# Down halves of the experts issued by ScalarE on a second hardware queue in a one-core decoder step

## The reference, cut to what matters

```
(jax.nn.silu(xb @ w_g[e]) * (xb @ w_u[e])) @ w_d[e]
```

## Time and profile before

| what | value |
|---|---|
| median of 3 runs | 2143.52 us (2139.1 to 2146.24) |
| the profiled execution: its own time | 2136.13 us |
| span of the profiled execution, first to last instruction | 2134.2 us |
| PE busy in the span | 1816.0 us, 85% |
| ACT busy in the span | 279.2 us, 13% |
| queue q1 (SP) | 520.24 MB, 64.1% of the 16 engines' span |
| queue q0 (software, POOL) | 17.05 MB, 2.3% |
| queue q10 (ACT) | 6.33 MB, 1.4% |

### The profile page before, as it was taken

How to read it: one execution, slowest core, us unless ns; L and a number is a source line. 1 busy time by engine, 2 the same in 40 slices (tenths; PEclk the granted TensorE clock), 3 DMA queues, 4 the chain that set the end, 5 groups by cost and what they waited for, 6 DMA issues and landing times.

```text
span 2134.2 us, 22022 instructions
## 1 busy us (share of the span) xinstructions
PE 1816.0 (85%) x8780; PEld 1134.8 (53%) x8780; DVE 614.8 (29%) x1129; ACT 279.2 (13%) x537; POOL 271.1 (13%) x188
## 2 busy tenths in 40 slices
PE   7798999998788999993999897979979887787770
PEld 6687888887367888882543433434334332232320
DVE  6900699652535400006401101011010110110116
ACT  4001211103641210013000000000000000000002
POOL 0641222211910100001000000000000000000000
PEclk9899999999999999995999999999999998999995
DMA  5144111345934243316399999999999999999957
GB/s 227 60 119 118 66 67 71 118 177 168 6 126 192 79 158 123 114 60 262 117 406 392 403 410 409 406 397 406 398 414 384 400 414 408 409 409 405 403 214 294
DMA packets 91139, 544.81 MB, mean 255 GB/s; under 512 B 27984, under 2 KB 40784, under 8 KB 44400
## 3 DMA queue, kind: packets, MB, share of 16 engines
q1 hardware_dynamic: 70512, 520.24, 64.1%
q0 software_dynamic: 5888, 17.05, 2.3%
q10 hardware_dynamic: 14656, 6.33, 1.4%
HBM read 522.81 MB, written 37.26 MB: 262 GB/s over the span
## 4 chain that ended last, share of the span: by engine, by line
PE 60%; DMA 25%; DVE 9%; ACT 4%; issue 1%; SPq 1%; ACTq 0%; POOL 0%; DVEq 0%; POOLq 0%
PE psum L570 30%; DMA arena<-w_up_in 22%; PE psum L897 8%; PE psum L862 7%; PE psum L855 4%; PE psum L858 4%; PE psum L838 2%; PE psum L664 1%; PE psum L776 1%; DMA arena<-y_rows 1%; DMA arena<-v_cache_in 1%; DVE arena L1662 1%; SPq L487 1%; DVE arena L1759 1%; DVE arena L1488 1%
## 5 line engine op out<-in xcount | busy, mean ns | idle before, releaser
L570 PE MATMUL psum<-arena 128*128 128x260 f32 x3328 | 746.5, 387 | 32.8 <-DVE arena L1293 14.7
L570 PEld LDWEIGHTS psum<-arena 128*128 128x128 f32 x3328 | 640.5, 193 | 135.5 <-issue 25.8
L862 PE MATMUL psum<-arena 128*64 128x512 f32 x832 | 402.6, 642 | 113.4 <-DMA arena<-w_up_in 113.3
L864 PE MATMUL psum<-arena 128*64 128x512 f32 x832 | 403.4, 643 | 0.0
L862 PEld LDWEIGHTS psum<-arena 128*64 128x64 f32 x832 | 119.5, 148 | 377.4 <-issue 377.4
L897 PE MATMUL psum<-arena 128*64 128x512 f32 (+1 forms) x1024 | 269.9, 597 | 17.7 <-ACT arena L1113 17.0
L897 PEld LDWEIGHTS psum<-arena 128*64 128x64 f32 (+1 forms) x1024 | 94.0, 147 | 170.8 <-issue 148.2
L1727 DVE TENSOR_TENSOR arena<-arena,psum 64x512 f32<-64x512 f32 x26 | 18.0, 691 | 493.5 <-ACT arena L1110 493.5
L1225 POOL DMA_INDIRECT y_rows<-arena x32 | 30.1, 941 | 990.4 <-DVE arena L1736 990.4
L1736 DVE COPY arena<-psum 64x512 f32<-64x512 f32 (+1 forms) x64 | 43.5, 687 | 274.8 <-PE psum L897 274.0
L864 PEld LDWEIGHTS psum<-arena 128*64 128x64 f32 x832 | 119.5, 148 | 0.0
(11 more groups left out here) (313 smaller groups left out, 1288.1 us busy)
## 6 DMA issues: line engine op xcount, KB each, us to landing
arena<-w_gate_in SPq DMA_DIRECT2D x64, 2048.0 KB, 38.3
arena<-w_up_in SPq DMA_DIRECT2D x64, 2048.0 KB, 42.2
arena<-w_down_in SPq DMA_DIRECT2D x64, 2048.0 KB, 41.2
arena<-w_in_in SPq DMA_DIRECT2D x32, 1024.0 KB, 4.8
arena<-w_out_in SPq DMA_DIRECT2D x16, 1024.0 KB, 4.7
arena<-k_cache_in SPq DMA_DIRECT2D x8, 1024.0 KB, 6.9
arena<-v_cache_in SPq DMA_DIRECT2D x8, 1024.0 KB, 4.8
arena<-y_rows SPq DMA_DIRECT2D x4, 2048.0 KB, 19.1
```

The costliest lines, as they stand in the source:

```text
L570: last = mm(pair(n)[:, h, :], w(kk), rhs(kk)[:, HALF * h:HALF * (h + 1)], start=(kk == first), stop=(kk == kn - 1 and stop))
L862: lastg = mm(ps[0:SLIM, 2, :], xt[:, 8 * hf + kk, :], wg[:, kk, :], start=(hf == 0 and kk == 0), stop=(hf == 1 and kk == 7))
L864: lastu = mm(ps[SLIM:P, 2, :], xt[:, 8 * hf + kk, :], wu[:, kk, :], start=(hf == 0 and kk == 0), stop=(hf == 1 and kk == 7))
```

## The change

The down halves of places 2 to 31 are no longer issued by SP. SP's loop issues only the gate and up halves (`range(4)` instead of `range(6)`). ACT gets a new function `load_down(i)`: it waits until the first gate and up halves of place i - 1 are used (`s_half`, the same condition as in `load_next`), loads the expert's number from `ord_i` into a register, and issues both down halves into the same ring slots as before, with the same semaphores. ACT calls it for place i + 1 at the start of its work on place i, ahead of the Silu of place i, and waits once for `s_ord` before its loop. Places 0 and 1 are loaded by SP as before, and the loads of overflow blocks too. Slots, sizes, sources and the order of use on PE are unchanged.

```diff
@@ SP
             for i in range(2, NE):
                 e = sp.value_load(ord_i[0:1, ORDER[i]:ORDER[i] + 1], min_val=0, max_val=NE - 1)
-                for j in range(6):
+                for j in range(4):
                     load_next(6 * i + j, e)
@@ ACT
+            def load_down(i):
+
+                slots = slots_of(i)[0]
+                act.wait_ge(s_half, i)
+                e = act.value_load(ord_i[0:1, ORDER[i]:ORDER[i] + 1], min_val=0, max_val=NE - 1)
+                src = t["w_down"][bass.ds(e, 1)].rearrange("o (k p) n -> p (o k) n", k=4)
+                for j in range(2):
+                    act.dma_start(half_d(slots[4 + j]), src[:, 2 * j:2 * j + 2, :]).then_inc(s_ring[slots[4 + j]], 16)
+
+            act.wait_ge(s_ord, 1)
             for i in range(NE):
+                if 2 <= i + 1 < NE:
+                    load_down(i + 1)
                 expert(i, WIDE[i])
             overflow(act, lambda it: expert(it + NE, True))
```

## The result

The changed kernel takes 2155.51 us (median of 5 runs, 2152.52 to 2159.46) against 2143.52 before: 12 us more by the medians. The ratio of the two sets of runs is 1.0061, 95% interval 1.004 to 1.0081, that is 13 us (8.6 to 17.4). The prediction was 2154, in a range of 2136 to 2169. The profiled execution took 2154.18 us; that of before, 2136.13, is among the quickest of its kernel, so the profiles differ by more (18 us) than the medians.

The account below looks back on a forecast made before the run. Transfers were taken to bound the kernel, with PE following. SP 0, ACT 0, order at the end +9.2 and clock +1.2 summed to +10.4 us, giving 2154 us from a median of 2143.5, range 2136 to 2169.

Parts of the forecast that it names:

- The bound: Expert part, 1060 to 2036 us: transfers are the limit, engines busy at share 1.01 and 404 GB/s, PE following.
- 1% mark: Expert part: the prediction would be wrong if the transfer rate moved by 1% or more.
- SP, 0: SP's loop: dropping 60 issues and 30 waits gains 0, as the queue behind is full.
- ACT, 0: ACT before each Silu: added wait, register load and two issues, 0.9 to 1.3 us, are covered, costing 0.
- The middle: Places before the end: down halves competing from q10 cost nothing that lasts, as late engines stay fed.
- Down halves land early by at most two halves: Middle places: so a pair comes at most 10.4 us later, which the ring's depth of about eight halves absorbs.
- The order at the tail, +9.2: Last place: the gate and up pair lands last, at 2066.0 instead of 2056.8 us, costing 9.2 us.
- once and not per place: Middle places: a pair's delay of at most 10.4 us arises a single time, without adding up over places.
- The clock, +1.2 out of 0 to 2.3: PE's restart at the last pair: slow clock after idling costs 0 to 2.3 us, taken as 1.2.
- Same: Rival at the end: the last pair does not land last, tail costs 0 to 6 us; chance 0.21.
- Faster: Rival in the expert part: two hardware queues raise the rate, 2125 us at 416 GB/s; chance 0.14.
- much slower: Rival in the expert part: two queues on an engine cost rate, 2189 us at 390 GB/s; chance 0.12.

Follow-up runs that it names:

- e9: Kernel before, ACT given only the change's waits and register loads, no issues, all halves on SP; 2142.84 us, 1.0003 of the kernel before.
- e3: Changed kernel, ACT also issuing the second gate and up pairs of places 2 to 31; 2149.95 us, 1.0019 of the kernel before.
- e6: Kernel before, ACT given the change's waits, register load and two tiny issues per place, all weights on SP; 2147.15 us, 1.0023 of the kernel before.
- e5: Kernel before, all on SP's one queue, last place's down halves issued ahead of its second pair; 2155.44 us, 1.0065 of the kernel before.
- e1: Changed kernel, but the last place's down halves issued by SP again, behind its gate and up halves; 2147.68 us, 1.0017 of the kernel before.
- e11: Kernel of e10 with the whole change on top; 2129.2 us, 0.9958 of the kernel before.
- e12: Kernel of e10 with the change for places 2 to 30, last place's down halves on SP; 2121.4 us, 0.9917 of the kernel before.
- e7: Changed kernel with four unused matmuls on PE ahead of the last place's second pair; 2154.14 us, 1.0058 of the kernel before.
- e10: Kernel before, rows of nine slim experts moved to positions and partitions 64 to 127, in lists of 128; 2112.31 us, 0.985 of the kernel before.
- e4: Changed kernel with nine unused matmuls on PE ahead of the last place's second pair; 2158.08 us, 1.0063 of the kernel before.

## Why the prediction held, and where it did not

- **The bound.** Right as a whole. The share stays at 1.00 and the rate of 401 GB/s is inside the 1% mark that I set; e9, which moves no transfer, has 402.
- **SP, 0.** Right: it is freed of its long issues and nothing gains from it. The rate does not gain by a second issuing engine either (401 GB/s, and 402 in e3, against 404). The order of arrival, taken from rows, was worth 9 us and more.
- **ACT, 0.** The two issues take 0.91 to 1.8 us, mostly 0.92 (0.9 to 1.3 expected), and are over 4 us or more before the next Silu. e9 shows no price of waits and register loads. e6 leaves up to 8 us in doubt for the issues, which the 0 did not allow for.
- **The middle.** The total came out as argued, but not quite for the reason given: the engines did not always stay fed (share 0.97 in 1460 to 1560 us), and down halves were awaited, 27.3 us, which I had named as a sign of being wrong. The step that failed is "Down halves land early by at most two halves". With a third of the time for q10 I had worked out 31 us for the two, and a place takes 31.1, so there was no air; they land after 33.9 us (median). Of the two values that I left open, a third or a half, the profile is nearer to the half where both queues have work: in 2036 to 2050 us q10 holds 51.7% of the engines' time and q1 47.4%. It cost little, a few us at most, for the transfers set the pace.
- **The order at the tail, +9.2.** Right in mechanism and size. e5 makes the loss by the order alone; taking one place out of the change wins back 0.44% (e1), 9.4 us, and e11 less e12 is 7.8. By landings the pair came 9.9 us ahead of the last down half before, 9.2 being read from the windows. The text held that a pair comes two halves later "once and not per place". The profiles of e1 and e12 suggest that this once is paid at whatever pair PE has too few waits left behind, so that sparing the last place does not make it free.
- **The clock, +1.2 out of 0 to 2.3.** Mis-sized in the profiled execution: the restart came at the upper bound, 2.3 us, after 4.42 us of idle. e7 shows the same 2.3 saved when PE is kept busy, but no run shows it in the medians. The slow down matmuls (1.6 us more) were not foreseen and are not the change's. The two profiles differ by 17.8 at the eviction, 4.7 of it from the end of the traffic and 3.9 from the clock, and both scatter between executions. That the sum of 10.4 meets the 12 of the medians within 2 us rests on their levelling out, to some 11 in the table, and is in part luck.
- **The rivals.** *Same* fell: the pair did land last, at 2070.7. *Faster* and *much slower* fell with a rate inside the 1% mark and, in the table above, a length of traffic that scatters alike on one queue and on two; e3, with twice the bytes on q10 and 1.0019 (0.9997 to 1.004), leaves a price for queues of 9 us at most.

## What to carry to other kernels

Where transfers set the pace, as here, a second issuing queue did not bring weights sooner (401 GB/s against 404); it changed which arrive first. At the end of a saturated stretch the halves that are used last should also land last, so that their transfer hides behind the work on the others; sending them ahead of the last pair cost 0.65% by itself (e5). Before splitting a queue, look at what the engines still move when the last needed piece has landed, and how many waits PE has left to absorb a shift. And read the end of such a stretch in windows of 2 us: engines that end at different times were the hint that led to e10, which was worth more than the order.

## What was not expected of the hardware

- The position of rows in the list of a gather or scatter matters to the traffic beside it: with 64-row lists filled from the front some engines ended 1 ms of saturated traffic 28 us after the others; other partitions made no difference (0.9995), other positions, in lists of 128, 1.5%. Positions that are skipped are still counted: q0 has 7040 packets instead of 5888, 1152 more, which is 9 experts x 64 positions x 2.
- The nine float32 matmuls of 512 columns of e4 ran as two passes each, some 0.44 us a pass (7.92 us for 18).
- After the same pause of 1.4 us between gate/up and down the granted clock sometimes dropped to the lower level and sometimes not (down 8.70 to 8.81 us, with 0.60 to 0.63 in its first half, or 7.11 us with 1.00), in kernels of equal time.
